# Two transformer blocks in one kernel: the order of work around the gated levels, the latents and the last heads

## The chip, the cores and the metric

One NeuronCore of a Trainium2 chip runs the whole program. It has a matrix engine (TensorE, PE in the profile, with the weight loads as PEld), a vector engine (VectorE, DVE), an activation engine (ScalarE, ACT), GpSimd (POOL) and the queue engine (SyncE, SP). The metric is device microseconds for one execution; lower is better.

## The reference

Two blocks run one after the other on a sequence of 512 tokens of width 1024, all in float32. The first is FFN, a mixer with two recurrences, FFN. The second is FFN, an attention mixer, FFN and a gated embedding. The parts that the change touches, cut from the reference:

```python
# first block, HGRN2 half: 4 heads of 128, chunks of 64
G = jnp.cumsum(gc, axis=2)                                   # log of the forget gates
o_inter = jnp.einsum("bhtk,bhkv->bhtv", qc * jnp.exp(G), S)
rel = G[:, :, :, None, :] - G[:, :, None, :, :]
decay = jnp.exp(jnp.where(causal, rel, -jnp.inf))
scores = jnp.sum(qc[:, :, :, None, :] * kc[:, :, None, :, :] * decay, axis=-1)
o = o_inter + jnp.einsum("bhts,bhsv->bhtv", scores, vc)
S_new = jnp.exp(G_end[:, :, 0, :])[..., None] * S + jnp.einsum("bhsk,bhsv->bhkv", kc * jnp.exp(G_end - G), vc)
...
# second block: latents, 8 softmax heads and 8 stick-breaking heads, branches
proj = u @ w_in[i]
c_q, c_kv, k_rope, sb_qkv, gates = jnp.split(proj, SPLITS, axis=-1)
q = (rms_norm_2(c_q, q_latent_norm[i]) @ w_q_up[i]).reshape(b, s, MLA_HEADS, MLA_QK)
kv = (rms_norm_2(c_kv, kv_latent_norm[i]) @ w_kv_up[i]).reshape(b, s, MLA_HEADS, MLA_NOPE + MLA_V)
o_mla = causal_softmax_attention(...)
o_sb = stick_breaking_attention(sq, sk, sv)
merged = g_mla * (o_mla @ w_branch_mla[i]) + g_sb * (o_sb @ w_branch_sb[i])
h = h + merged @ w_out[i]
```

## The kernel before

**Weights and products.** Every dense product is done as three matmuls on float32r halves (`mm3`: high by high, low by high, high by low). SyncE loads 512 KB pieces of weights ("chunks") into three raw buffers. GpSimd splits each into a high and a low part (`pool_split`, L343 and L345) as soon as TensorE has used up the chunk three places ahead. Each engine's program is written out by hand, in one fixed order, and the engines meet at counting semaphores (`wait_ge`, `then_inc`). A dense product of one chunk is 24 matmuls of 512 columns (L380 to L382).

**The levels of the first mixer.** The decay inside a chunk of 64 steps is cut into seven levels (`level(0)` to `level(6)` on TensorE, L608). Level n reads one of three work buffers, `g.item(n + 1)`. For items 2 to 7 DVE writes the exponents' arguments (`exponents`, L1898 and L1899), ACT takes the exponential (`exponent`, L1379), and DVE multiplies by q and k (`multiply`, L1909 and L1910). After the level's matmuls DVE picks the wanted scores out of PSUM (`keep`, L1920). Between the levels TensorE does the mixer's other dense products (`fill`), and `kv(0, 1)`, `kv(2, 3)`, `kv(4, 5)`, `kv(6)` (L632), the updates of the state. `kv(2, 3)` writes the banks that DVE empties in `remember(0)` and `remember(1)` (L1928, L1933), and waits for both. ACT takes each fill's result out of PSUM (`take`, L1367) between its exponentials, in a fixed order.

**The latents.** The second mixer's input product has 34 chunks (`for i in range(2, 34)` on TensorE, banks 4 to 7 in turn); DVE scales each result into SBUF (L2185). Chunks 0 to 2 are the query latent and 3 and 4 the key and value latent. Their norms need squares (ACT, L1506), sums over partitions on TensorE (`pe_latent_sums`, L816, which waits for each tile of squares), a root and a reciprocal, then a scaled and split copy (`latent_hi` on ACT, L1510). Chunks 18 to 33 are the gates, to which ACT applies a sigmoid (`gate`, L1514).

**The heads.** For each pair of heads TensorE makes stick-breaking logits and sums (L958, L960, L977), softmax logits (L1010), transposes of the divided probabilities (L1022), and the products with the values: `values(h, m)` (L1039 for stick-breaking head h into bank 7, L1042 for softmax head m into bank 6). An odd head uses the upper 64 partitions of its bank, an even one the lower 64. In the loop it is called with m = h - 1; at the end `values(None, 6)` and `values(7, 7)` stand alone. GpSimd divides the probabilities of each head by their row sums (L361). DVE copies the outputs out of PSUM (`stick_out` L2328, `mla_out` L2332). When both heads of a pair are out, ACT makes the high part (L1662) and GpSimd the low part (L355) of the pair's tile for the branch products; DVE makes the low parts of the last two (`last_pairs`, L2346). `pe_merge` then multiplies the eight tiles by each of the 8 branch chunks.

Of the kernel before, what the change touches and what calls it, by code (L numbers as in the profile page):

```python
# [10 lines left out]
ACT = mybir.ActivationFunctionType  # L11
# [3 lines left out]
P = 128  # L15
T = 512
NT = T // P
D = 1024
KD = D // P
# [13 lines left out]
AH = 8  # L33
NOPE, ROPE, QK, HV = 64, 32, 96, 64
KCQ, KCKV = 3, 2
# [207 lines left out]
def tile(t, i):  # L243
    return t[:, i * T:(i + 1) * T]
# [103 lines left out]
def pool_attend(k):  # L348

    pool, H = k.nc.gpsimd, Heads(k)  # L350

    def pairs(h):
        for n in COMPLETE.get(h, ()):
            pool.wait_ge(k.pair_hi, KD + PAIRS.index(n) + 1)
            pool.tensor_tensor(tile(k.ulo, n), H.o[n], tile(k.uhi, n).bitcast(F32), ALU.subtract).then_inc(k.pair_lo, 1)  # L355

    for h in range(AH):
        pool.wait_ge(k.rs_inv, h + 1)
        for i, c in ROWS:
            w = H.probs[:, c:c + (i + 1) * P]  # L360
            d = pool.tensor_scalar(w, w, H.rs[:, h * NT + i:h * NT + i + 1], None, ALU.mult)  # L361
        d.then_inc(k.divided, 1)
        pairs(h)


# [418 lines left out]
def pe_attention_mixer(k):  # L784
    pe = k.nc.tensor
    pe_enter(k, 4, "proj_in")
    for i in range(2, 34):
        if i >= 4:
            pe.wait_ge(k.proj_scaled, i - 3)
        pe_dense(k, "proj_in", i, CHUNK_BANK[i % 4])  # L790
        if i == 8:
            pe_latent_sums(k, 0, KCQ, 0)
        elif i == 11:
            pe_turn_key_rope(k)
        elif i == 18:
            pe_latent_sums(k, KCQ, KCKV, 1)
        elif i == 21:
            pe.wait_ge(k.proj_scaled, 11)
            pe.wait_ge(k.norm_var, NORM["kl"])
            pe.wait_ge(k.kr_step, 1)  # L800
            pe.wait_ge(k.masks_done, 3)
            pe_stick_logits(k, 0)
        elif i == 27:

            pe.wait_ge(k.z_copied, 1)
            pe_turn(k, k.big[:, 14 * T:18 * T], 0, 4 * NT)
    pe_make_heads(k)
    pe_attend(k)
    pe_merge(k)
# [98 lines left out]
def half(h):  # L908
    return slice(h % 2 * HV, (h % 2 + 1) * HV)
# [55 lines left out]
def pe_attend(k):  # L965
# [59 lines left out]
    def values(h, m):  # L1025

        if h is not None:
            pe.wait_ge(k.z_weights, h + 1)
            if h:
                pe.wait_ge(k.z_out, h)  # L1030
        if m is not None:
            pe.wait_ge(k.p_copied, m + 1)
            if m:
                pe.wait_ge(k.o_out, m)
        last = len(CAUSAL_BLOCKS) - 1
        for n, (i, t0, width, c) in enumerate(CAUSAL_BLOCKS):
            if h is not None:
                v = H.sv[:, ((h // 2) * NT + i) * P + h % 2 * HV:((h // 2) * NT + i) * P + (h % 2 + 1) * HV]
                z = pe.matmul(k.ps[7][half(h), t0:t0 + width], v, H.z_at(h, c, width), start=n == 0, stop=n == last, skip_group_check=True)  # L1039
            if m is not None:  # L1040
                v = H.v[:, (m * NT + i) * HV:(m * NT + i + 1) * HV]
                o = pe.matmul(k.ps[6][half(m), t0:t0 + width], v, H.turned_at(m, c, width), start=n == 0, stop=n == last, skip_group_check=True)  # L1042
        if h is not None:
            z.then_inc(k.z_values, 1)
        if m is not None:
            o.then_inc(k.o_values, 1)
# [17 lines left out]
    values(AH - 1, AH - 1)  # L1064


def turned_bank(h):

    return B0 if h < AH - 1 else A0


def pe_merge(k):
    pe = k.nc.tensor
    for j in range(KD):
        n, hi, lo = k.pair("branch", j)
        pe.wait_ge(k.w_split, 2 * n + 2)
        b = 2 * (j % 2)
        if j >= 2:
            pe.wait_ge(k.merge_dve, 3 * (j - 2) + 2)
        else:  # L1080
            pe.wait_ge(k.p_copied, AH)
        for part in (1, 0):
            for t in range(4):
                kk = 4 * part + t
                if j == 0:
                    pe.wait_ge(k.pair_hi, KD + PAIRS.index(kk) + 1)
                    if kk in COMPLETE[AH]:
                        pe.wait_ge(k.last_lo, COMPLETE[AH].index(kk) + 1)
                    else:
                        pe.wait_ge(k.pair_lo, KD + PAIRS.index(kk) + 1)  # L1090
                m = mm3(pe, k.ps[b + part], hi, lo, slice(kk * P, (kk + 1) * P), tile(k.uhi, kk), tile(k.ulo, kk), t == 0, t == 3)
        m.then_inc(k.w_used, 1)

    def ready(kk):
        pe.wait_ge(k.merge_lo, kk + 1)

    def free(i):
        if i == 0:
            pe.wait_ge(k.p_copied, AH)
        elif i == 1:  # L1100
            pe.wait_ge(k.z_out, AH)
            pe.wait_ge(k.o_out, AH)
        else:
            pe.wait_ge(k.merge_dve, 3 * (4 + i) + 2)

    pe_out(k, 4, "proj_out", KD, lambda kk: tile(k.hhi, kk), lambda kk: tile(k.hlo, LO_AT + kk), ready, free, (0, 1, 2, 3))
# [390 lines left out]
def act_attention_mixer(k):  # L1497
# [19 lines left out]
    act_root(k, "ql", k.sc[3][:, :])  # L1517
    for n in range(KCQ):
        latent_hi(n)
    gate(18)  # L1520
    latent_squares(KCQ, KCKV)
    gate(19)
    act_root(k, "kl", k.sc[3][:, :])
    latent_hi(KCQ)
    gate(20)
    latent_hi(KCQ + 1)
    for i in range(21, 34):
        gate(i)
        if i == 21:
# [89 lines left out]
def act_attend(k):  # L1619
# [36 lines left out]
    def pairs(h):  # L1656
        for n in COMPLETE.get(h, ()):
# [3 lines left out]
                act.wait_ge(k.z_out, 2 * n - 6)  # L1661
            act.copy(tile(k.uhi, n), H.o[n]).then_inc(k.pair_hi, 1)  # L1662

    act.preload_act_table_set("natural_log_exp_and_others")
    exponents(0)
    for h in range(1, AH):
        stick_logits(h)
        weigh(h - 1)
        exponents(h)
        act_soft_hi(k, h)  # L1670
        pairs(h)
    weigh(AH - 1)
    pairs(AH)
# [171 lines left out]
def dve_gated_mixer(k):  # L1845
# [108 lines left out]
    dve.wait_ge(k.qf_taken, 8)  # L1954
    dve.tensor_tensor(g.item(1), q, kk, ALU.mult).then_inc(k.level_mul, 1)
    multiply(KEYS_ITEM)
    for n in range(last + 1):
        multiply(n + 2)
        keep(n)
        if n + 3 < QUERIES_ITEM:  # L1960
            exponents(n + 3)
        if n >= 4:
            remember(2 * (n - 4))
            remember(2 * (n - 4) + 1)
# [202 lines left out]
def dve_attention_mixer(k):  # L2167
# [14 lines left out]
    for i in range(34):  # L2182
# [4 lines left out]
        if i == 9:  # L2187
            latent_norm("ql", 0, KCQ, 0)
            latent(0, "q_latent", 0)
        elif i == 10:  # L2190
            latent(1, "q_latent", 1)
            latent(2, "q_latent", 2)
        elif i == 13:
            dve_key_rope(k)
        elif i == 15:
            dve_masks(k)
        elif i == 19:
            latent_norm("kl", KCQ, KCKV, 1)
            latent(3, "kv_latent", 0)
        elif i == 20:  # L2200
            latent(4, "kv_latent", 1)
        elif i == 25:
            dve_softplus(k, 0)
# [93 lines left out]
def dve_attend(k):  # L2297
# [31 lines left out]

    def mla_out(h):  # L2330
        dve.wait_ge(k.o_values, h + 1)
        dve.tensor_copy(H.o[h // 2][half(h), :], k.ps[6][half(h), :]).then_inc(k.o_out, 1)  # L2332

    def split(h):
        dve.wait_ge(k.soft_hi, h + 1)
# [7 lines left out]
    def last_pairs():  # L2343
        for n in COMPLETE[AH]:
            dve.wait_ge(k.pair_hi, KD + PAIRS.index(n) + 1)
            dve.tensor_tensor(tile(k.ulo, n), H.o[n], tile(k.uhi, n).bitcast(F32), ALU.subtract).then_inc(k.last_lo, 1)  # L2346

    split(0)
    maxima(0)
    divide(0)  # L2350
    for h in range(1, AH):
        add_sums(h - 1)
# [207 lines left out]
```

## Time and profile before

| What | Value |
|---|---|
| Time of one execution, median of 3 runs | 2257.95 us (2257.26 to 2259.03) |
| Time of the profiled execution | 2261.95 us |
| Its span | 2260.6 us |
| TensorE busy (matmuls) | 2215.2 us, 98% of the span |
| TensorE weight loads busy | 1832.6 us, 81% |
| GpSimd busy | 1315.4 us, 58% |
| VectorE busy | 828.1 us, 37% |
| ScalarE busy | 452.4 us, 20% |
| Granted TensorE clock, mean | 0.994 |

The span is what the profiler saw between the first and the last instruction; the time of the same execution is 1.35 us more. TensorE is nearly always busy, so the rows that count are those that stand between two of its matmuls, and the stretches in which its granted clock is below 1.00. A row of the timeline gives start, length, engine, line, what it does, and in square brackets how long the engine had been idle before it and who ended that.

### The profile page before, as it was taken

The numbers are of one execution on the slowest core, as the hardware profiler recorded it, in microseconds if no ns is written. First come the engines' busy times: TensorE is split into PE (matmuls) and PEld (weight loads), VectorE is DVE, ScalarE is ACT, GpSimd is POOL, SyncE is SP. The second block draws the span as 40 slices with busy tenths as digits, with TensorE's granted clock in tenths as the row PEclk, the third lists the DMA queues.
The fourth block names the chain that finished last, engine by engine and source line by source line (L and its number), as shares of the span: only waits on it lengthen the run. The fifth ranks groups of instructions, "written<-read, shape, count | busy, mean of one in ns | idle before, by whom it ended". The sixth has DMA issues, their size and how long they took to land.

```text
span 2260.6 us, 25908 instructions
## 1 busy us (share of the span) xinstructions
PE 2215.2 (98%) x10938; PEld 1832.6 (81%) x10938; DVE 828.1 (37%) x929; ACT 452.4 (20%) x751; POOL 1315.4 (58%) x772
## 2 busy tenths in 40 slices
PE   8999999989999999999999999999999999999999
PEld 7888888867788888888888888878767888888887
DVE  3334203776443333104443202143566633333013
ACT  3111004323331111003111102013476121111012
POOL 5666664634356666665666665656435656666654
PEclk9999999999999999999999999999999999999999
DMA  5232322212222323232322322222200323323222
GB/s 182 94 102 93 98 98 75 94 48 66 66 84 99 97 93 102 94 96 82 103 94 95 101 93 94 88 90 84 78 1 20 93 84 100 96 94 111 93 86 92
DMA packets 55819, 200.84 MB, mean 89 GB/s; under 512 B 6680, under 2 KB 6808, under 8 KB 55576
## 3 DMA queue, kind: packets, MB, share of 16 engines
q1 hardware_dynamic: 53856, 194.14, 26.7%
q10 hardware_dynamic: 1848, 5.04, 0.6%
q8 instruction: 87, 1.43, 0.3%
q14 instruction: 28, 0.23, 0.0%
HBM read 197.06 MB, written 2.10 MB: 88 GB/s over the span
## 4 chain that ended last, share of the span: by engine, by line
PE 74%; DVE 2%; ACT 1%; issue 1%; POOL 0%; DVEq 0%; ACTq 0%
PE psum L380 15%; PE psum L382 15%; PE psum L381 15%; PE psum L462 7%; PE psum L463 7%; PE psum L461 7%; PE psum L1010 1%; PE psum L960 1%; PE psum L977 1%; PE psum L425 1%; PE psum L1128 1%; PE psum L1130 1%; PE psum L1129 1%; ACT work L1646 0%; PE psum L668 0%
## 5 line engine op out<-in xcount | busy, mean ns | idle before, releaser
L345 POOL TENSOR_TENSOR w_lo<-w_raw,w_hi 128x1024 fp32r<-128x1024 f32 x365 | 884.2, 2422 | 30.4
L343 POOL TENSOR_SCALAR w_hi<-w_raw 128x1024 fp32r<-128x1024 f32 x365 | 387.3, 1061 | 828.1 <-PE psum L382 573.1
L380 PE MATMUL psum<-u_hi,w_hi 128*128 128x512 f32 (+1 forms) x2072 | 792.8, 383 | 1.9 <-DVE u_lo L1747 1.1
L381 PE MATMUL psum<-u_hi,w_lo 128*128 128x512 f32 (+1 forms) x2072 | 787.9, 380 | 0.0
L382 PE MATMUL psum<-u_lo,w_hi 128*128 128x512 f32 (+1 forms) x2072 | 787.7, 380 | 0.0
L380 PEld LDWEIGHTS psum<-u_hi,w_hi 128*128 128x128 f32 x2072 | 391.6, 189 | 79.2 <-issue 4.7
L382 PEld LDWEIGHTS psum<-u_lo,w_hi 128*128 128x128 f32 x2072 | 391.1, 189 | 74.0
L381 PEld LDWEIGHTS psum<-u_hi,w_lo 128*128 128x128 f32 x2072 | 391.3, 189 | 73.7 <-issue 0.8
L461 PE MATMUL psum<-w_hi,hidden_hi 128*128 128x512 f32 x800 | 311.4, 389 | 0.9 <-DVE work L2099 0.9
L462 PE MATMUL psum<-w_lo,hidden_hi 128*128 128x512 f32 x800 | 311.2, 389 | 0.0
L463 PE MATMUL psum<-w_hi,hidden_lo 128*128 128x512 f32 x768 | 298.8, 389 | 0.0
L1834 DVE TENSOR_TENSOR hidden_lo<-scratch,hidden_hi 128x512 fp32r<-128x512 f32 x88 | 238.3, 2708 | 60.7 <-ACT hidden_hi L1334 60.7
L1832 DVE TENSOR_TENSOR scratch<-scratch,psum 128x512 f32<-128x512 f32 x88 | 60.5, 688 | 404.1 <-PE psum L382 398.9
L461 PEld LDWEIGHTS psum<-w_hi,hidden_hi 128*128 128x128 f32 x800 | 150.1, 188 | 32.6 <-DVE work L2099 1.3
L462 PEld LDWEIGHTS psum<-w_lo,hidden_hi 128*128 128x128 f32 x800 | 150.2, 188 | 31.1
L463 PEld LDWEIGHTS psum<-w_hi,hidden_lo 128*128 128x128 f32 x768 | 144.1, 188 | 29.8
L1334 ACT CAST hidden_hi<-scratch 128x512 fp32r<-128x512 f32 x88 | 54.8, 623 | 406.9 <-DVE scratch L1832 406.9
L1332 ACT ACTIVATE scratch<-scratch 128x512 f32<-128x512 f32 x88 | 55.6, 632 | 394.0 <-DVE scratch L1826 393.9
L1826 DVE TENSOR_TENSOR scratch<-psum,diag 128x512 f32<-128x512 f32 x88 | 60.9, 692 | 121.8 <-PE psum L382 99.9
L1787 DVE SCALAR_TENSOR_TENSOR x<-psum,misc,x 128x1024 f32<-128x1024 f32 x8 | 10.3, 1284 | 223.2 <-PE psum L463 223.1
L1769 DVE SCALAR_TENSOR_TENSOR psum<-psum,misc,post_gain 128x1024 f32<-128x1024 f32 x8 | 10.3, 1293 | 217.3 <-ACT junk L1240 217.0
L1206 ACT ACTIVATE junk<-x 128x1024 bf16<-128x1024 f32 x28 | 29.5, 1052 | 263.5 <-DVE x L1787 252.9
(287 smaller groups left out, 1549.1 us busy)
## 6 DMA issues: line engine op xcount, KB each, us to landing
w_raw<-in_ffn_in SPq DMA_DIRECT2D x176, 512.0 KB, 3.4
w_raw<-in_ffn_out SPq DMA_DIRECT2D x88, 512.0 KB, 3.4
w_raw<-in_proj_in SPq DMA_DIRECT2D x34, 512.0 KB, 3.4
w_raw<-in_mix_in SPq DMA_DIRECT2D x29, 512.0 KB, 3.3
w_raw<-in_embed SPq DMA_DIRECT2D x10, 512.0 KB, 3.5
w_raw<-in_mix_out SPq DMA_DIRECT2D x8, 512.0 KB, 3.4
w_raw<-in_branch SPq DMA_DIRECT2D x8, 512.0 KB, 3.5
w_raw<-in_proj_out SPq DMA_DIRECT2D x8, 512.0 KB, 3.5
```

What stands on the lines that cost most here:

```text
L343: pool.tensor_scalar(hi, raw, 1.0, 1.0, ALU.mult, ALU.mult).then_inc(k.w_split, 1)
L345: pool.tensor_tensor(lo, raw, hi.bitcast(F32), ALU.subtract).then_inc(k.w_split, 1)
L380: pe.matmul(out, hi[:, cols], xhi, start=first, stop=False)
L381: pe.matmul(out, lo[:, cols], xhi, start=False, stop=False)
L382: return pe.matmul(out, hi[:, cols], xlo, start=False, stop=last)
L461: pe.matmul(bank, xhi(kk)[:, tokens], hi[:, cols], start=kk == 0, stop=False)
L462: pe.matmul(bank, xhi(kk)[:, tokens], lo[:, cols], start=False, stop=False)
L463: return pe.matmul(bank, xlo(kk)[:, tokens], hi[:, cols], start=False, stop=last)
L1332: act.activation(sg, sg, ACT.Silu).then_inc(k.silu_done, 1)
L1826: dve.tensor_tensor(sg, k.ps[CHUNK_BANK[2 * i % 4]], k.diag[:, :], ALU.mult).then_inc(k.gate_scaled, 1)
L1832: dve.tensor_tensor(hm, sg, k.ps[CHUNK_BANK[(2 * i + 1) % 4]], ALU.mult).then_inc(k.multiplied, 1)
L1834: dve.tensor_tensor(tile(k.hlo, i), hm, tile(k.hhi, i).bitcast(F32), ALU.subtract).then_inc(k.hid_lo, 1)
```

## The change

Line numbers of the profile are those of the kernel before. Seven edits:

1. DVE writes the exponents' arguments of item n + 3 before it multiplies item n + 2 (from n = 1 on), where it did so after `keep(n)`.
2. The key and value latent's sums on TensorE move from behind chunk 18 to behind chunk 12. On ACT its squares, root and high parts stand together ahead of the gates 18 to 20. On DVE its norm moves from chunk 19 and 20 to chunk 17 and 18.
3. The division of the last softmax head (7) moves from GpSimd to ACT.
4. The last softmax head's output goes to the lower half of bank 5 instead of the upper half of bank 6, so `values(7, 7)` no longer waits for the copy of head 6.
5. `pe_merge` takes the tiles in the order 4, 5, 6, 0, 1, 2, 7, 3 instead of 4, 5, 6, 7, 0, 1, 2, 3.
6. The output product that follows waits for the last head's copy out of bank 5 before it writes there.
7. DVE takes head 0's row maxima before the low part of head 0's sums.

```diff
@@ pool_attend
     for h in range(AH):
-        pool.wait_ge(k.rs_inv, h + 1)
-        for i, c in ROWS:
-            w = H.probs[:, c:c + (i + 1) * P]
-            d = pool.tensor_scalar(w, w, H.rs[:, h * NT + i:h * NT + i + 1], None, ALU.mult)
-        d.then_inc(k.divided, 1)
+
+        if h < AH - 1:
+            pool.wait_ge(k.rs_inv, h + 1)
+            for i, c in ROWS:
+                w = H.probs[:, c:c + (i + 1) * P]
+                d = pool.tensor_scalar(w, w, H.rs[:, h * NT + i:h * NT + i + 1], None, ALU.mult)
+            d.then_inc(k.divided, 1)
         pairs(h)
@@ pe_attention_mixer
-        elif i == 18:
+        elif i == 12:
             pe_latent_sums(k, KCQ, KCKV, 1)
@@ pe_attend, values
             pe.wait_ge(k.p_copied, m + 1)
-            if m:
+            if 0 < m < AH - 1:
                 pe.wait_ge(k.o_out, m)
...
-                o = pe.matmul(k.ps[6][half(m), t0:t0 + width], v, H.turned_at(m, c, width), start=n == 0, stop=n == last, skip_group_check=True)
+                o = pe.matmul(softmax_out(k, m)[:, t0:t0 + width], v, H.turned_at(m, c, width), start=n == 0, stop=n == last, skip_group_check=True)
...
+def softmax_out(k, m):
+
+    return k.ps[6][half(m), :] if m < AH - 1 else k.ps[5][half(0), :]
@@ pe_merge
-        for part in (1, 0):
-            for t in range(4):
-                kk = 4 * part + t
...
+        for kk in (4, 5, 6, 0, 1, 2, 7, 3):
+            part, t = kk // 4, kk % 4
...
     def free(i):
         if i == 0:
-            pe.wait_ge(k.p_copied, AH)
+            pe.wait_ge(k.o_out, AH)
@@ act_attention_mixer
-    gate(18)
     latent_squares(KCQ, KCKV)
-    gate(19)
     act_root(k, "kl", k.sc[3][:, :])
-    latent_hi(KCQ)
-    gate(20)
-    latent_hi(KCQ + 1)
+    for n in range(KCKV):
+        latent_hi(KCQ + n)
+    for i in range(18, 21):
+        gate(i)
@@ act_attend
+    def divide(h):
+        act.wait_ge(k.rs_inv, h + 1)
+        for i, c in ROWS:
+            w = H.probs[:, c:c + (i + 1) * P]
+            a = act.activation(w, w, ACT.Copy, scale=H.rs[:, h * NT + i:h * NT + i + 1])
+        a.then_inc(k.divided, 1)
...
         act_soft_hi(k, h)
+        if h == AH - 1:
+            divide(h)
         pairs(h)
@@ dve_gated_mixer
-    for n in range(last + 1):
+    multiply(2)
+    keep(0)
+    exponents(3)
+    for n in range(1, last + 1):
+        if n + 3 < QUERIES_ITEM:
+            exponents(n + 3)
         multiply(n + 2)
         keep(n)
-        if n + 3 < QUERIES_ITEM:
-            exponents(n + 3)
         if n >= 4:
             remember(2 * (n - 4))
             remember(2 * (n - 4) + 1)
@@ dve_attention_mixer
-        elif i == 19:
+        elif i == 17:
             latent_norm("kl", KCQ, KCKV, 1)
             latent(3, "kv_latent", 0)
-        elif i == 20:
+        elif i == 18:
             latent(4, "kv_latent", 1)
@@ dve_attend
     def mla_out(h):
         dve.wait_ge(k.o_values, h + 1)
-        dve.tensor_copy(H.o[h // 2][half(h), :], k.ps[6][half(h), :]).then_inc(k.o_out, 1)
+        dve.tensor_copy(H.o[h // 2][half(h), :], softmax_out(k, h)).then_inc(k.o_out, 1)
...
+    maxima(0)
     split(0)
-    maxima(0)
     divide(0)
```

What the edits move, engine by engine. VectorE at the levels, before: items are told apart by the shape of their rows, 512x2 is item 3, 256x4 is item 4, 128x8 is item 5; L1898 and L1899 write arguments, L1909 and L1910 multiply, L1920 keeps.

```order
L1898 TENSOR_TENSOR work<-work 128x512x2
L1899 TENSOR_TENSOR work<-work 128x512x2
L1909 TENSOR_TENSOR work<-work 128x512x2
L1910 TENSOR_TENSOR work<-work 128x512x2
L1920 COPY_PREDICATED scratch_f_72<-const,psum 128x1024
L1898 TENSOR_TENSOR work<-work 128x256x4
L1899 TENSOR_TENSOR work<-work 128x256x4
L1909 TENSOR_TENSOR work<-work 128x256x4
L1910 TENSOR_TENSOR work<-work 128x256x4
```

The same place of the changed kernel, where the lines are L1913 and L1914 (arguments), L1924 and L1925 (multiply) and L1935 (keep):

```order
L1913 TENSOR_TENSOR work<-work 128x512x2
L1914 TENSOR_TENSOR work<-work 128x512x2
L1913 TENSOR_TENSOR work<-work 128x256x4
L1914 TENSOR_TENSOR work<-work 128x256x4
L1924 TENSOR_TENSOR work<-work 128x512x2
L1925 TENSOR_TENSOR work<-work 128x512x2
L1935 COPY_PREDICATED scratch_f_72<-const,psum 128x1024
L1913 TENSOR_TENSOR work<-work 128x128x8
L1914 TENSOR_TENSOR work<-work 128x128x8
L1924 TENSOR_TENSOR work<-work 128x256x4
L1925 TENSOR_TENSOR work<-work 128x256x4
```

The arguments of item 4 now stand ahead of the product of item 3, those of item 5 ahead of that of item 4, and so on to item 7.

ScalarE at the latents, before: L1510 is a high part, L1514 a gate, L1506 a square, L1192 the root.

```order
L1510 CAST hidden_lo<-work 128x512 x3
L1514 ACT_TABLE_LOAD
L1514 ACTIVATE work<-work 128x512
L1506 ACTIVATE scratch_66<-work 128x512
L1506 ACTIVATE scratch_67<-work 128x512
L1514 ACTIVATE work<-work 128x512
L1192 ACT_TABLE_LOAD
L1192 ACTIVATE scratch_68<-scratch_68 128x512
L1510 CAST hidden_lo<-work 128x512
L1514 ACT_TABLE_LOAD
```

In the changed kernel (L1517 a high part, L1513 a square, L1199 the root, L1521 a gate):

```order
L1517 CAST hidden_lo<-work 128x512 x3
L1513 ACTIVATE scratch_66<-work 128x512
L1513 ACTIVATE scratch_67<-work 128x512
L1199 ACTIVATE scratch_68<-scratch_68 128x512
L1517 CAST hidden_lo<-work 128x512 x2
L1521 ACT_TABLE_LOAD
L1521 ACTIVATE work<-work 128x512 x4
```

The two squares no longer stand behind gate 18, and two table loads are gone.

ScalarE at the last heads, before: L1616 is the high part of head 7's sums, L1662 the high part of a pair, L1653 the stick-breaking weights of head 7.

```order
L1616 CAST split_sums_63<-scratch_f_72 128x1280
L1662 CAST u_hi<-work 128x512 x2
L1653 ACTIVATE work<-work 128x1280
L1662 CAST u_hi<-work 128x512 x2
```

In the changed kernel (L1622, L1668 and L1659 are those three, L1674 is new):

```order
L1622 CAST split_sums_63<-scratch_f_72 128x1280
L1674 ACTIVATE work<-work,misc 128x512
L1674 ACTIVATE work<-work,misc 128x384
L1674 ACTIVATE work<-work,misc 128x128
L1674 ACTIVATE work<-work,misc 128x256
L1668 CAST u_hi<-work 128x512 x2
L1659 ACTIVATE work<-work 128x1280
L1668 CAST u_hi<-work 128x512 x2
```

Four divisions have come in between the head's sums and the pairs; on GpSimd the four L361 of head 7 are gone.

## Rows read from the trace of the kernel before

**Rows 1.** Waits of TensorE: total us, times, longest.

```profile
PE psum L632 <- DVE work L1933: 5.4, 1, 5.4
...
PE psum L816 <- ACT scratch L1506: 2.0, 1, 2.0
```

**Rows 2.** Timeline of TensorE at the levels: start, us, instruction, idle before.

```profile
463.57 2.09 PE L608 MATMUL psum<-work 128*64 128x64 f32 x64 [3.09 <-DVE work L1910]
...
489.86 2.08 PE L632 MATMUL psum<-work 64*128 64x128 f32 x16 [5.42 <-DVE work L1933]
```

**Rows 3.** Timeline of VectorE at the levels.

```profile
453.83 3.38 DVE L1898 TENSOR_TENSOR work<-work 128x1024 f32<-128x1024 f32 x1
...
460.32 1.23 DVE L1909 TENSOR_TENSOR work<-work 128x1024 f32<-128x1024 f32 x1 [1.98 <-ACT work L1379]
461.46 2.06 DVE L1910 TENSOR_TENSOR work<-work 128x1024 f32<-128x1024 f32 x1
463.44 1.36 DVE L1920 COPY_PREDICATED scratch_f<-const,psum 128x1024 f32<-128x1024 uint32 x1
...
484.63 3.36 DVE L1899 TENSOR_TENSOR work<-work 128x1024 f32<-128x1024 f32 x1
...
488.68 1.12 DVE L1933 SCALAR_TENSOR_TENSOR work<-work,misc,psum 128x128 f32<-128x128 f32 x4
```

**Rows 4.** Timeline of GpSimd beside it.

```profile
453.74 2.38 POOL L345 TENSOR_TENSOR w_lo<-w_raw,w_hi 128x1024 fp32r<-128x1024 f32 x1
```

**Rows 5.** Timeline of ScalarE beside it.

```profile
452.47 0.59 ACT L1367 COPY work<-psum 128x512 f32<-128x512 f32 x1 [2.20 <-PE psum L382]
458.37 1.92 ACT L1379 ACTIVATE work<-work 128x2048 f32<-128x2048 f32 x1 [5.31 <-DVE work L1899]
```

**Rows 6.** Windows of TensorE: us, busy (instructions), granted clock, DMA share, GB/s.

```profile
489.00:496.00 7.00, 6.14 (x26) 0.51 0.09 36
1516.00:1520.00 4.00, 4.00 (x10) 0.57 0.38 131
```

**Rows 7.** Timelines of TensorE, ScalarE and VectorE at the latents.

```profile
1515.17 2.54 PE L816 MATMUL psum<-scratch,const 128*128 128x512 f32 x4 [1.97 <-ACT scratch L1506]
...
1479.11 0.62 ACT L1510 CAST hidden_lo<-work 128x512 fp32r<-128x512 f32 x1 [4.38 <-DVE work L2177]
...
1480.37 1.28 DVE L2185 SCALAR_TENSOR_TENSOR work<-psum,diag 128x512 f32<-128x512 f32 x2
```

**Rows 8.** Timeline of TensorE at the heads 6 and 7.

```profile
1729.55 0.32 PE L1039 MATMUL psum<-work 128*64 128x128 f32 x1
...
1731.66 0.27 PE L1042 MATMUL psum<-work 128*64 128x128 f32 x1
...
1737.46 1.31 PE L1022 MATMUL psum<-const,work 128*128 128x128 f32 x10 [1.09 <-POOL work L361]
1738.70 2.38 PE L1042 MATMUL psum<-work 128*64 128x128 f32 x14
1741.95 0.40 PE L1039 MATMUL psum<-work 128*64 128x128 f32 x2 [0.86 <-DVE work L2332]
...
1746.40 0.50 PE L380 MATMUL psum<-u_hi,w_hi 128*128 128x512 f32 x1
...
1748.59 0.40 PE L380 MATMUL psum<-u_hi,w_hi 128*128 128x512 f32 x1
```

**Rows 9.** Timelines of GpSimd, ScalarE and VectorE beside it.

```profile
1732.79 4.62 POOL L361 TENSOR_SCALAR work<-work,misc 128x512 f32<-128x512 f32 x4 [5.74 <-DVE misc L2341]
...
1733.02 0.64 ACT L1662 CAST u_hi<-work 128x512 fp32r<-128x512 f32 x1
...
1737.93 1.27 ACT L1653 ACTIVATE work<-work 128x1280 f32<-128x1280 f32 x1 [1.14 <-DVE work L2303]
...
1739.95 0.42 DVE L2323 COPY diag<-psum 128x256 f32<-128x256 f32 x1
...
1747.67 1.30 DVE L2346 TENSOR_TENSOR u_lo<-work,u_hi 128x512 fp32r<-128x512 f32 x2
```

More of the change, by code:

```diff
@@ L1081, in pe_merge @@
             pe.wait_ge(k.p_copied, AH)
-        for part in (1, 0):
-            for t in range(4):
-                kk = 4 * part + t
[L1085 to L1091, printed above, removed]
+        for kk in (4, 5, 6, 0, 1, 2, 7, 3):
+            part, t = kk // 4, kk % 4
+            if j == 0:
+                pe.wait_ge(k.pair_hi, KD + PAIRS.index(kk) + 1)
+                if kk in COMPLETE[AH]:
+                    pe.wait_ge(k.last_lo, COMPLETE[AH].index(kk) + 1)
+                else:
+                    pe.wait_ge(k.pair_lo, KD + PAIRS.index(kk) + 1)
+            m = mm3(pe, k.ps[b + part], hi, lo, slice(kk * P, (kk + 1) * P), tile(k.uhi, kk), tile(k.ulo, kk), t == 0, t == 3)
         m.then_inc(k.w_used, 1)
```

## The prediction

> **What bounds the kernel now.** TensorE's matmuls fill 98% of the span, so a change of order can win only what lies between them: waits, and matmuls at the lower clock. I read the waits of TensorE first. In the mixer of the first block one wait of 5.4 us stands out, in front of `kv(2, 3)`; in the second block the longest that this change touches is the 2.0 us in front of the latent sums [rows 1]. Then the timeline of TensorE around them. At the levels it waits 3.09 us for the product of item 4 before `level(3)` at 463.57, and 5.42 us for `remember(1)` before 489.86 [rows 2]. At the last heads it waits 1.09 us for GpSimd's division and 0.86 us for the copy of head 6, and its last pair of products is slow (below) [rows 8]. Third, the windows: after the 5.42 us and after the 1.97 us the granted clock is 0.51 and 0.57, so the engine mostly works at 1.2 instead of 2.4 GHz though it is busy again [rows 6]. The reader is to see that each of these waits costs its own length, and two of them matmuls at half speed behind it.
>
> **Edit 1, arguments ahead of the product.** Before, DVE writes the arguments of an item, then sits idle 1.98 us while ACT takes the exponential, then multiplies [rows 3]. ACT starts when the arguments are there, 458.37 for item 4, though it has been free since 453.06, when it had emptied the fill's bank [rows 5]. With the arguments ahead, those of item 4 are written in the idle time of item 3, which is as long. No split of GpSimd falls there, so two pieces of 1.23 us, overlapped to some 1.15 each (460.32 to 461.46 in the same rows), take 2.3 us in place of 1.98: the product of item 3 ends 0.35 us later, and `level(2)` starts as much later. That is the price. ACT then takes item 4 at 453.06 and is done at 455.0. The arguments of item 5 come next on DVE and meet GpSimd's split of a chunk.
>
> Here VectorE and GpSimd are to be read together [rows 3, 4]: an argument piece that takes 1.21 to 1.23 us alone takes 3.38 us when it starts 0.09 us behind L345 (453.74, 2.38 us long): 2.29 us until that one ends and then its own time, near enough. The split ends at 456.12 plus the shift of 0.35, so the arguments of item 5 end at 456.5 + 2 x 1.2 = 458.9 and the product of item 4 at 461.2, not 463.52. TensorE is ready for `level(3)` at 463.57 - 3.09 + 0.35 = 460.83 and waits about 0.4 us. It starts at 461.2: 2.4 us won. If the two engines shared instead of excluding each other, the arguments, begun at 454.2, would end a microsecond or more sooner, `level(3)` would wait nothing, and the win would be 3.09 - 0.35 = 2.7 us. The Trainium skill, page "SBUF — State Buffer", section on the shared port pair, says that a DVE instruction with two SBUF inputs and a GpSimd one that reads SBUF exclude each other for the whole instruction. It speaks against this edit, since it puts two more such instructions in front of each product; by that rule, the trace agrees and the 2.4 stands.
>
> Next `kv(2, 3)`. It waits for DVE, whose list from 461.2 on is: keep, arguments 6, product 5, keep, arguments 7, product 6, keep, `remember(0)`, `remember(1)`. Dear prices: keep 1.3 (three times), arguments 4.6 (3.38 + 1.23, twice), products 2.3 (twice), `remember(0)` 0.7 (484.63 + 3.36 to 488.68), `remember(1)` 1.1 [rows 3]. Sum 19.5, so 480.7. One product stretched to 3.2 (as in 460.32 to 463.52) gives 481.6. TensorE comes to `kv(2, 3)` at 489.86 - 5.42 - 2.4 = 482.0. The wait is gone with 0.4 to 1.3 us to spare, more if the arguments don't meet a split. So 5.4 us are won, and with them the stretch at half clock: of 489 to 496, 6.14 us were busy at 0.51, and lose 6.14 x 0.49 = 3.0 us [rows 6]. Levels 4 to 6 have their products 1 to 3 us before TensorE is there by the same list. Behind `kv(4, 5)` everything hangs on ACT's bank copies and on TensorE itself, in the same order as before. Edit 1: 2.4 + 5.4 + 3.0 = **10.8 us**.
>
> **Edit 2, latents.** The squares stood behind gate 18 on ACT, which needs chunk 18; TensorE waited for them for 1.97 us and then worked 4.00 us at 0.57 [rows 6, 7]. The second cost is 4.00 x 0.43 = 1.7 us. Now ACT makes them right behind its third high part, from 1479.73 (1479.11 + 0.62); the first is there at 1480.4. TensorE ends chunk 12 at about the time at which DVE is through with chunk 11 and takes 12, 1480.5 to 1481 [rows 7], so it waits 0 to 0.3 us; take 0.1. The sums themselves only move. DVE has the norm two chunks earlier; it will be some 5 us behind with chunk 18, and TensorE asks for that only three chunks later. Gates 18 to 20 come late on ACT, which sat idle most of this stretch. Edit 2: 1.97 + 1.7 - 0.1 = **3.6 us**. If the cover fails (third high part late by the 2.3 us of one split), the wait is back whole: nothing won, bound 0.
>
> **Edits 3 to 6, last heads.** Transposes of head 7: GpSimd's divisions run 1732.79 to 1737.41 [rows 9]; TensorE would be ready at 1737.46 - 1.09 = 1736.37 [rows 8]. On ACT four instructions follow L1616. ACT has no such division in the trace. Below, one instruction of 1280 columns took 1.27 us; above, four times the 0.64 of a 512-column one is 2.6 [rows 9]. I take 1.8, as most of the four are shorter. From 1733.1 that ends at 1734.9, and even the upper bound, 1735.7, is ahead of 1736.37. So 1.09 us go. What ACT holds back by it: pair tile 6, whose low part GpSimd now makes sooner than before, being free of 4.62 us. Then `values(None, 6)` ends at 1740.0, and `values(7, 7)` needs no copy of head 6: weights are there at 1739.2 (1737.93 + 1.27) and the turned probabilities at 1739.3 (1740.37 less the 1.09), so 0.86 us go.
>
> The pair itself: of heads 6 and 5 the 28 matmuls run from 1729.55 to 1731.93, two by two at the same instant, since one head writes the lower and one the upper half of its bank. Those of `values(7, 7)` both write an upper half and run one behind the other from 1741.95 to 1746.40: 4.45 us against 2.38 [rows 8]. With head 7's softmax output in a lower half the pair takes 2.4 us: 2.05 us go. Sum 1.09 + 0.86 + 2.05 = **4.0 us**, and the branches begin at 1742.4.
>
> The Trainium skill, page "TensorE: Matmul & The Clock Gate", Part 3 on packing small matmuls, "What overlaps and what doesn't", would have a weight load overlap a running matmul only if the two use different row groups. Here both heads use all 128 rows, so by that rule the pair would stay at 4.45 us and this part would give 1.95. The trace disagrees: 14 matmuls alone (L1042 at 1738.70) take 2.38 us, as long as the 28 of the pair before.
>
> The branches need tile 7. Its low part followed the last value product by 1.9 us (L2346 at 1747.67, two in 1.30, against 1746.40) [rows 8, 9], and three tiles take 2.2 (1746.40 to the tenth matmul at 1748.59): in the old order it would be a matter of 0.3 us. The new order has six tiles, 4.4 us, ahead of it; even if a GpSimd split of 2.4 us blocks the subtraction it is just there. Edit 5 gives nothing itself, but covers this. Edit 6 waits for something long done. Edit 7: the maxima come a microsecond sooner, but ACT loads a table at that time, so 0.
>
> **Sum.** 10.8 + 3.6 + 4.0 = 18.4 us, from the profiled execution's 2261.95 to 2243.6. The three timed runs have their median 4.0 us below the profiled one, which leaves 2239.6. Part of that 4.0 may be just half-clock stretches, which the timed runs then can't give back; the 1.7 us of the latents followed a wait so short that I count half of it. That and small waits that a list worked out misses make me say **2241 us**.
>
> **The rivals.** (a) As above, 2236 to 2245: chance 0.70. (b) DVE is late after all at `kv(2, 3)`: two products stretched (1.0 us each) and one more argument piece blocked (3.38 for 1.23) take 480.7 to 484.9, a wait of 2.9 us, and the half clock comes back with 3.0 us. That is 2247; for it speaks the slack of 0.4 to 1.3 us, against it that GpSimd has one split of 3.4 us per chunk and can't block every piece. Chance 0.14. (c) The pair of the last heads does not run side by side, or a wait for the copy from the lower to the upper half takes its place: 2.05 us less, 2243; chance 0.05. (d) The latent part does nothing, since the third high part is late, or the clock falls elsewhere instead: 3.5 us less, 2244.5; chance 0.07. (e) The other side: DVE becomes last at each of the levels 2 to 6. Its place is the arguments in front of each product. The price is their whole length, up to 4.6 us, five times, 23 us, and one half-clock stretch of 3.0: 2241 + 26 = 2267. It decides, that is, the kernel is measurably slower, from (2258 + 4.5 - 2241 - 3.0)/5 = 3.7 us per level. Against it: the exponential and DVE's idle 1.98 us per item leave the chain at the same time, and the split blocks one or two pieces per chunk. Chance 0.02. (f) Nothing of it shows, since the waits move to a place that I don't see: 2258; chance 0.02.
>
> **How the numbers follow.** A measurement of this kernel can tell about 0.2%, 4.5 us, from no change. (a) to (d) lie beyond it, which is 0.96; a quarter of a part of (b) and (d) together would fall short, 0.02. So faster 0.94, same 0.04, slower 0.02. The range holds (a), (c), (d) and most of (b): 2235.5 to 2247.5.
>
> **What would show it.** In the profile of the changed kernel: DVE's arguments two rows ahead of the product; no idle time of DVE for the exponential at items 4 to 7; `level(3)` with a wait below 0.5 us; no wait at L632, granted clock 1.00 for the ten microseconds behind it; the latent sums without a wait behind chunk 12; the transposes of head 7 and `values(7, 7)` without waits and the latter's 28 matmuls in 2.4 us; no gap in the first branch product. I am wrong if a wait of more than 2 us stands at L608 or L632 in the levels, or if half-clock stretches as long in sum as before appear elsewhere.

## The result and the profile after

The changed kernel takes 2240.76 us, the median of 4 runs (2239.35 to 2244.82), against 2257.61 us for the kernel before in the same session (2257.18 to 2259.03): ratio 0.9927, 95% interval 0.991 to 0.9944. That is 16.9 us less; the forecast was 2241, with a range of 2235.5 to 2247.5. The profiled execution took 2244.82 us with a span of 2243.5 us, so it is 4.1 us longer than the median.

The page of the changed kernel, first its engines. TensorE is busy 4.0 us less than before, the span is 17.1 us shorter.

```profile
PE 2211.2 (99%) x10938; PEld 1831.7 (82%) x10938; DVE 825.5 (37%) x929; ACT 451.0 (20%) x753; POOL 1314.8 (59%) x768
```

Waits of TensorE in the changed kernel, as [rows 1]. Of the waits that the prediction names, one short one at the levels (L610) is left; those in front of `kv(2, 3)` (now L634), the latent sums (L818), head 7's transposes (L1024) and `values(7, 7)` (L1041) have no row any more.

```profile
PE psum L610 <- DVE work L1925: 0.5, 1, 0.5
```

Timeline of TensorE at the levels, as [rows 2]: levels 2 and 3, `kv(2, 3)`, and L649, the first product behind the levels, which in the kernel before (L647) began at 514.97.

```profile
453.10 2.08 PE L610 MATMUL psum<-work 128*64 128x64 f32 x64 [0.48 <-DVE work L1925]
460.96 2.08 PE L610 MATMUL psum<-work 128*64 128x64 f32 x64
...
481.75 1.16 PE L634 MATMUL psum<-work 64*128 64x128 f32 x16
...
504.07 1.09 PE L649 MATMUL psum<-work,scratch_f 64*64 64x128 f32 x16
```

Timeline of VectorE there, as [rows 3].

```profile
454.24 3.26 DVE L1913 TENSOR_TENSOR work<-work 128x1024 f32<-128x1024 f32 x1
...
458.56 1.21 DVE L1924 TENSOR_TENSOR work<-work 128x1024 f32<-128x1024 f32 x1
459.70 1.21 DVE L1925 TENSOR_TENSOR work<-work 128x1024 f32<-128x1024 f32 x1
...
473.49 1.86 DVE L1924 TENSOR_TENSOR work<-work 128x1024 f32<-128x1024 f32 x1 [1.45 <-ACT work L1386]
...
478.42 1.13 DVE L1948 SCALAR_TENSOR_TENSOR work<-work,misc,psum 128x128 f32<-128x128 f32 x4
482.27 2.28 DVE L1924 TENSOR_TENSOR work<-work 128x1024 f32<-128x1024 f32 x1 [2.73 <-ACT work L1386]
```

Of the arguments of item 5, the first piece (L1913) takes 3.26 us. The product of item 4 (L1924, L1925) stands directly behind them and ends at 460.91; TensorE takes it at 460.96 without a wait. `remember(1)` (L1948) is done at 479.55 and TensorE comes to `kv(2, 3)` at 481.75, 2.2 us later. For items 6 and 7 VectorE still waits for the exponential. Why, the timeline of ScalarE shows:

```profile
468.75 0.59 ACT L1374 COPY work<-psum 128x512 f32<-128x512 f32 x1 [5.46 <-PE psum L384]
469.24 1.08 ACT L1391 COPY work<-psum 128x512 f32<-128x512 f32 x2
...
471.55 1.92 ACT L1386 ACTIVATE work<-work 128x2048 f32<-128x2048 f32 x1
...
479.84 0.59 ACT L1374 COPY work<-psum 128x512 f32<-128x512 f32 x1 [6.24 <-PE psum L384]
480.32 1.92 ACT L1386 ACTIVATE work<-work 128x2048 f32<-128x2048 f32 x1
```

ScalarE starts each exponential (L1386) only when it has emptied the bank of TensorE's fill (L1374), which stands ahead of it in its list; for item 6 four further copies (L1391) stand there too. The arguments are there before that. So ScalarE now waits for TensorE and VectorE for ScalarE; TensorE waits for neither.

At the latents and the heads of the changed kernel, timeline of TensorE, as [rows 7, 8]. The sums run without a wait; the products of `values(7, 7)` (L1041 and L1044, one of each shown) run side by side, and the branches begin at 1729.31.

```profile
1471.00 1.89 PE L818 MATMUL psum<-scratch,const 128*128 128x512 f32 x4
...
1720.86 2.92 PE L979 MATMUL psum<-split_sums,sums_lhs 128*128 128x512 f32 x18 [1.33 <-ACT split_sums L1622]
1723.62 1.28 PE L1024 MATMUL psum<-const,work 128*128 128x128 f32 x10
1724.83 2.27 PE L1044 MATMUL psum<-work 128*64 128x128 f32 x13
...
1728.57 0.27 PE L1041 MATMUL psum<-work 128*64 128x128 f32 x1
1728.67 0.27 PE L1044 MATMUL psum<-work 128*64 128x128 f32 x1
...
1729.31 0.50 PE L382 MATMUL psum<-u_hi,w_hi 128*128 128x512 f32 x1
```

Windows of TensorE in the changed kernel, as [rows 6]: behind level 3, and behind `kv(2, 3)`. Both are at full clock.

```profile
463.50:469.50 6.00, 6.00 (x31) 1.00 0.01 3
488.00:494.00 6.00, 6.00 (x93) 1.00 0.12 27
```

### The profile page after: what moved, and what is told of

Read it like the earlier page. It is cut to its first block, busy times and chain, and to the rows that moved or that the text cites. A ratio compares the mean times of both kernels' runs of the same rounds, so it can differ in the third digit from the quotient of the medians.

```text
span 2243.5 us, 25905 instructions
## 1 busy us (share of the span) xinstructions
PE 2211.2 (99%) x10938; PEld 1831.7 (82%) x10938; DVE 825.5 (37%) x929; ACT 451.0 (20%) x753; POOL 1314.8 (59%) x768
## 4 chain that ended last, share of the span: by engine, by line
PE 93%; DVE 4%; ACT 2%; issue 1%; DMA 0%; POOL 0%; SPq 0%; DVEq 0%; ACTq 0%
PE psum L382 20%; PE psum L384 19%; PE psum L383 19%; PE psum L463 8%; PE psum L464 8%; PE psum L465 8%; PE psum L1012 1%; PE psum L979 1%; PE psum L962 1%; PE psum L427 1%; PE psum L1135 1%; PE psum L1137 1%; PE psum L1136 1%; ACT work L1652 1%; PE psum L610 0%
## 5 line engine op out<-in xcount | busy, mean ns | idle before, releaser
L345 POOL TENSOR_TENSOR w_lo<-w_raw,w_hi 128x1024 fp32r<-128x1024 f32 x365 | 888.2, 2433 | 30.4
```

The lines of the kernel that those rows point to most:

```text
L345: pool.tensor_tensor(lo, raw, hi.bitcast(F32), ALU.subtract).then_inc(k.w_split, 1)
```

## The experiments

The sessions of these runs had medians of 2255.4 to 2257.8 us for the kernel before, and one of them a single run of it at 2254.2. The changed kernel itself was not timed again in them: where a time is set against its 2240.76 us, the two come from different sessions, and a difference of 1 or 2 us between such times shows nothing by itself. Where a stage is compared, its length is read from the trace, since the time of a whole execution also holds half-clock stretches that fall in other places each time (see below).

**Edit 1 undone** in the changed kernel.

```diff
-    multiply(2)
-    keep(0)
-    exponents(3)
-    for n in range(1, last + 1):
+    for n in range(last + 1):
+        multiply(n + 2)
+        keep(n)
         if n + 3 < QUERIES_ITEM:
             exponents(n + 3)
-        multiply(n + 2)
-        keep(n)
```

> The changed kernel with edit 1 alone undone: each item's arguments are written after keep again. If the levels carry 10.8 us as the sum says (2.4 at level 3, 5.4 at kv(2, 3), 3.0 of clock), the time rises from 2240.8 to about 2251.5, with a wait near 3 us at level 3, near 5.4 us at kv(2, 3) and a granted clock near 0.5 behind it. If the clock part is not the wait's doing, both waits come back but only 7.8 us: 2248.5. If the gain came from somewhere else, under 2 us come back.

Measured: 2254.09 us, median of 9 (2244.61 to 2254.88), so 13.3 come back by the medians, where the sum said 10.8. The traced execution was at 2247.33, one of the shorter ones. TensorE's timeline there:

```profile
463.57 2.64 PE L610 MATMUL psum<-work 128*64 128x64 f32 x64 [3.09 <-DVE work L1925]
...
488.19 1.60 PE L634 MATMUL psum<-work 64*128 64x128 f32 x16 [2.19 <-DVE work L1948]
...
512.04 1.09 PE L649 MATMUL psum<-work,scratch_f 64*64 64x128 f32 x16
```

and its windows:

```profile
463.50:469.50 6.00, 5.93 (x74) 0.72 0.29 90
```

The 3.09 us are back, but the 5.42 us are only 2.19. The granted clock fell already behind the wait at level 3 (and again behind `kv(2, 3)`, 0.72 from 488 to 494). That made TensorE 1.5 us later at level 4 (475.12 against 473.59), and with it GpSimd's splits, which follow TensorE. So the split that meets item 7's arguments began 0.18 us behind the first of them, where in the kernel before its second part (L345, 483.72) had begun 0.91 us ahead of the second of them. Timelines of VectorE and GpSimd there:

```profile
483.97 1.21 DVE L1913 TENSOR_TENSOR work<-work 128x1024 f32<-128x1024 f32 x1
...
484.15 3.07 POOL L343 TENSOR_SCALAR w_hi<-w_raw 128x1024 fp32r<-128x1024 f32 x1 [6.76 <-PE psum L384]
```

Now the split is the one that is late, with 3.07 us for a part that takes 1.05 elsewhere, and the arguments took 1.21 and 1.22 us where the second had taken 3.36 [rows 3]. Of the 3.2 us by which the wait is shorter, 1.6 are TensorE's being later and 1.7 VectorE's being sooner (`remember(1)` done at 488.13 against 489.80). The size of this wait is not the program's alone.

**Edit 1 alone** in the kernel before (the same diff the other way).

> The kernel before with edit 1 alone. By the sum 10.8 us less than before, 2257.6 to 2246.8, with no wait at kv(2, 3). If the edits need each other, that is, if the clock or a wait goes only when all are there, the gain is below 8 us: above 2249.5.

Measured: 2247.94 us (2247.79 to 2252.53, 4 runs) against 2257.4, ratio 0.9954 (0.9938 to 0.997): 9.5 us less, no wait at `kv(2, 3)`, L647 at 504.26. The edit needs no other.

**Only `remember` earlier** in the kernel before: it frees what `kv(2, 3)` waits for, but overlaps nothing with the exponential.

```diff
         keep(n)
-        if n + 3 < QUERIES_ITEM:
-            exponents(n + 3)
         if n >= 4:
             remember(2 * (n - 4))
             remember(2 * (n - 4) + 1)
+        if n + 3 < QUERIES_ITEM:
+            exponents(n + 3)
```

> The kernel before, with only remember(0) and remember(1) put ahead of the arguments of items 7 in the list of VectorE; every argument still follows its keep. If the 5.4 us at kv(2, 3) and the 3.0 us of clock behind it are a matter of where remember stands, and the overlap with the exponential is worth only the 2.4 us at level 3, this gives most of the other 8.4: about 2249 to 2251, with the 3.09 us at level 3 left. If the overlap is what frees kv(2, 3), the wait is still above 3 us and the time is within 2 us of before, or a wait for item 7 takes its place at level 6.

Measured: 2257.41 us (11 runs) against 2257.78 (15 runs), ratio 0.9994 (0.9983 to 1.0006): nothing. Its waits at L632 and the next level:

```profile
485.56 1.16 PE L632 MATMUL psum<-work 64*128 64x128 f32 x16 [0.87 <-DVE work L1933]
492.94 2.09 PE L608 MATMUL psum<-work 128*64 128x64 f32 x64 [0.56 <-DVE work L1910]
496.43 1.16 PE L632 MATMUL psum<-work 64*128 64x128 f32 x16 [1.40 <-DVE work L1933]
```

The one wait became three, 2.83 us together. VectorE's list is as long as before, with its idle 1.98 us per item, and what is moved forward makes the next item late. By the medians the theory that the place of `remember` carries 8.4 us fell. Its trace says less against it: the clock stayed full behind level 3, and L647 began at 509.94, that is 5.0 us ahead of the one trace of the kernel before with full clock there (514.97) and 5.9 us behind the changed kernel. In such an execution the overlap carries only the larger part of the gain. Why the medians show none of the 5.0 us is open.

**The kernel before, two more traces**, and **edit 1 undone, a second trace.**

> The kernel before once more, unchanged, for a second trace of it. In the trace of the prediction TensorE waited 5.42 us at kv(2, 3) and lost 3.0 us of clock behind it; in the changed kernel with the levels as before it waited 2.19 us there, after a half-clock stretch behind the wait at level 3. If the wait is fixed by the program, it is 5.4 us here too and the time near 2261. If it depends on where a half-clock stretch happens to fall, a shorter wait shows with a stretch between 464 and 469 us, and the time is near the median, 2257.5.

> The kernel before a third time, for the same question: either 5.4 us at kv(2, 3) with full clock behind level 3, or about 2.2 us with a half-clock stretch behind level 3. A third pattern would speak against both.

> The changed kernel with edit 1 undone, a second trace. Five of its nine executions lay at 2254 to 2255 us, the traced one at 2247.3 with 2.19 us at kv(2, 3). If the long executions are those with the long wait, this run is either near 2254 with 5.4 us at kv(2, 3), or near 2247 with 2.2 us. If it is near 2254 with 2.2 us, the difference lies in half-clock stretches elsewhere in the program.

Measured: 2254.54, 2257.91 and 2245.05 us. TensorE in the second trace of the kernel before (wait at level 3, `kv(2, 3)`, and the end of the levels):

```profile
463.91 3.58 PE L608 MATMUL psum<-work 128*64 128x64 f32 x64 [3.09 <-DVE work L1910]
...
488.47 1.16 PE L632 MATMUL psum<-work 64*128 64x128 f32 x16 [2.19 <-DVE work L1933]
...
510.80 1.09 PE L647 MATMUL psum<-work,scratch_f 64*64 64x128 f32 x16
```

and its windows at level 3:

```profile
463.50:469.50 6.00, 5.59 (x73) 0.72 0.29 90
```

The third trace has the same two waits and a second stretch, 0.72 from 488 to 494; its L647 began at 512.42. In the second trace of the kernel with edit 1 undone, the stretch behind level 3 is longer and the wait at `kv(2, 3)` is gone altogether:

```profile
463.94 3.68 PE L610 MATMUL psum<-work 128*64 128x64 f32 x64 [3.11 <-DVE work L1925]
...
487.30 1.16 PE L634 MATMUL psum<-work 64*128 64x128 f32 x16
...
509.62 1.09 PE L649 MATMUL psum<-work,scratch_f 64*64 64x128 f32 x16
```

Its windows at level 3:

```profile
463.50:469.50 6.00, 5.56 (x69) 0.50 0.29 90
```

In both further traces of the kernel before, too, the split began 0.16 to 0.17 us behind the first arguments of item 7 and was the one held off, and they took 1.21 or 1.22 us each. So the old order has no single price. Its first product behind the levels began at 514.97, 512.04, 510.80, 512.42 and 509.62 in five traces (mean 511.97), that of the new order at 503.92 to 504.55 in eight (504.07 in the changed kernel's own). Edit 1 is worth 5.5 to 10.9 us in these traces, 7.9 on average; the trace that the prediction rests on is the worst of the five. The 7.9 is an average of five traces and not of all executions: the times give 9.5 us for the edit alone and 13.3 for undoing it, and both traces with it undone are of its shorter executions. What remains open is why five of the nine executions of the first experiment lay at 2254 to 2255 us; their mean granted clock is 0.994, against 0.996 in both traced ones, but none of them was traced.

**Edit 2 undone**, and **only the place of the sums as before** (TensorE behind chunk 18, norm at chunks 19 and 20, but ScalarE's order as changed).

```diff
-        elif i == 12:
+        elif i == 18:
             pe_latent_sums(k, KCQ, KCKV, 1)
...
```

> The changed kernel with edit 2 alone undone: sums behind chunk 18, squares behind gate 18. The wait of 1.97 us comes back. If the clock falls with it, as in the kernel before (4.00 us at 0.57), 3.6 us come back: 2244.4; if not, 2.0: 2242.8. The rival that the latents gave nothing says 2240.8.

> The changed kernel with the latent sums of TensorE back behind chunk 18 and the norm back at chunks 19 and 20, but ScalarE's squares still ahead of its gates. If the gate ahead of the squares made the wait, there is none here and the time is that of the changed kernel, 2240.8, within 1. If the place of the sums matters, 2 to 3.6 us come back.

Measured: 2245.66 us (2243.07 to 2248.25, 4 runs) with edit 2 undone, 2240.68 (2237.63 to 2241.01, 5 runs) with only the sums moved back. In the first, TensorE's timeline at the sums:

```profile
1499.31 3.55 PE L818 MATMUL psum<-scratch,const 128*128 128x512 f32 x4 [1.96 <-ACT scratch L1513]
```

and the windows there (us; busy of TensorE, its weight loads, VectorE, ScalarE and GpSimd; granted clock; DMA share; GB/s):

```profile
1499.00:1504.00 5.00, 4.69 (x10) 2.42 (x11) 0.00 (x0) 0.77 (x2) 1.99 (x1) 0.66 0.32 105
```

The wait and the half clock come back together (5.00 x 0.34 = 1.7 us). In the second, ScalarE's timeline has the squares done long before, and TensorE has no wait for them behind chunk 18:

```profile
1466.62 0.62 ACT L1517 CAST hidden_lo<-work 128x512 fp32r<-128x512 f32 x1 [4.40 <-DVE work L2195]
1467.14 1.15 ACT L1513 ACTIVATE scratch<-work 128x512 f32<-128x512 f32 x2
```

The gate ahead of the squares was the whole cause; the move of the sums adds nothing to it. In all six traces with the old order the wait of 1.96 to 1.97 us had a half-clock stretch behind it, in none of the eight others is there one between 1465 and 1520 us. From the first L825 (L827 in the changed kernel) to the first L958 (L960) the six take 60.50 to 60.61 us and the eight 56.67 to 56.71, whether the sums stand behind chunk 18 (56.69) or 12. This part is worth 3.9 us in every traced execution, not in some. Edit 7 was not undone by itself, but other traces can tell: from the first L958 (L960) to head 0's first sum (L977, L979) it is 110.3 us in two traces without the edit (edit 1 alone, the second trace of the kernel before) and in two with it (only the sums moved back, edit 5 undone), all at full clock there. It gives nothing.

**Edits 3 to 6 undone**, then one at a time: GpSimd divides head 7 (edit 3 undone), and head 7's output in an upper half.

```diff
-    return k.ps[6][half(m), :] if m < AH - 1 else k.ps[5][half(0), :]
+    return k.ps[6][half(m), :] if m < AH - 1 else k.ps[5][half(1), :]
```

> The changed kernel with edits 3 to 6 undone. By the sum 4.0 us come back (1.09 at the transposes, 0.86 at the last pair of values, 2.05 because that pair runs one behind the other): 2244.8. The rival that the half of the bank does not matter says 1.95 us: 2242.7.

> The changed kernel with edit 3 alone undone: GpSimd divides head 7. By the sum TensorE waits about 1.1 us again at the transposes of head 7, and 1.1 us come back: 2241.9. If GpSimd's low part of pair 6 then comes late as well, a further wait stands at the branches, up to 2 us more. The rival that ScalarE's division gains nothing says 2240.8.

> The changed kernel, with the last softmax head's output in the upper half of bank 5 instead of the lower. Both heads of the last pair then write upper halves. If the halves decide whether the 28 matmuls run side by side, they take 4.4 us instead of 2.4, and 2.0 us come back: 2242.8. If a weight load overlaps a running matmul only for another row group, the halves do not matter and the time stays 2240.8 with the pair at 2.4 us in both.

Measured: 2243.56 us (2242.08 to 2245.12, 4 runs), 2243.3 (2239.31 to 2247.09, 5 runs) and 2241.62 (2241.21 to 2243.67, 5 runs). These medians lie 2.8, 2.5 and 0.9 us above the changed kernel's, from another session, and the executions scatter by as much as is asked for, so the stage is read: from the first sum of head 7 (L979) to the first branch product. In the changed kernel it is 1729.31 - 1720.86 = 8.45 us. With all undone it is 1726.59 - 1713.46 = 13.13, 4.7 us more; with GpSimd dividing 1728.00 - 1718.10 = 9.90, 1.45 more; with the upper half 10.52, 2.07 more. TensorE in the latter:

```profile
1715.20 2.93 PE L979 MATMUL psum<-split_sums,sums_lhs 128*128 128x512 f32 x18 [1.34 <-ACT split_sums L1622]
...
1725.19 0.38 PE L1041 MATMUL psum<-work 128*64 128x128 f32 x2
1725.41 0.38 PE L1044 MATMUL psum<-work 128*64 128x128 f32 x2
1725.72 0.50 PE L382 MATMUL psum<-u_hi,w_hi 128*128 128x512 f32 x1
```

One head's two matmuls take 0.22 us here and then the other's, where in the changed kernel the two heads start 0.10 us apart and each issues one every 0.11 us. Nothing but the half of the bank differs, and the pair's end is 2.07 us later: the half decides.

**Edit 5 undone.**

```diff
-        for kk in (4, 5, 6, 0, 1, 2, 7, 3):
+        for kk in (4, 5, 6, 7, 0, 1, 2, 3):
```

> The changed kernel with edit 5 alone undone: the branches take tile 7 fourth. The prediction called its cover a matter of 0.3 us, which would give 2241.1. The trace of the changed kernel says more: GpSimd's split of 2.39 us lies ahead of the low parts of the last two tiles, so that of tile 7 is there some 4.0 us after the branches begin, while three tiles take 2.2 us: a wait of about 1.8 us in the first branch product, 2242.6.

Measured: 2242.87 us (2242.71 to 2243.81, 5 runs), 2.1 more than the changed kernel in its session. TensorE's timeline there, in the first branch product:

```profile
1729.49 0.47 PE L382 MATMUL psum<-u_hi,w_hi 128*128 128x512 f32 x1 [1.61 <-DVE u_lo L2364]
```

VectorE's, with the low parts of the last two tiles:

```profile
1726.96 2.98 DVE L2364 TENSOR_TENSOR u_lo<-work,u_hi 128x512 fp32r<-128x512 f32 x2
```

and GpSimd's:

```profile
1726.41 2.38 POOL L345 TENSOR_TENSOR w_lo<-w_raw,w_hi 128x1024 fp32r<-128x1024 f32 x1
```

The low parts start 0.55 us behind a split's second part, and TensorE waits for that of tile 7. In the kernel before the two took 1.30 us [rows 9]. The first branch product, from its first matmul to that of the next one, takes 7.48 us here (1725.52 to 1733.00) and 5.57 in the changed kernel (1729.31 to 1734.88): edit 5 is worth 1.9 us. Counted from the first sum of head 7, the splits begin at 4.75 us in the changed kernel (1725.61 - 1720.86) and at 6.59 with edits 3 to 6 undone (1720.05 - 1713.46), 1.8 us earlier; the branches begin 4.7 us earlier. So edits 3 to 6 bring the low parts 2.9 us nearer, into the second split, and edit 5 covers that.

## Why the prediction was right, and where its steps were off

**The time was right, its make-up less so.** The sum of 18.4 us was 10.8 + 3.6 + 4.0. By the stages it is 7.9 on average + 3.9 + 4.7 = 16.5 us, against 16.9 by the medians. Edit 1 was taken 2.9 us too large against that average, edits 2 to 6 by 1.0 us too small. The prediction took 1.4 us off its gain between the sum (2239.6) and 2241, partly for a reason that does not hold (below). That errors of both signs met within 0.3 us of the median is luck.

**Edit 1: the mechanism right, its size that of one execution.** At level 3 the forecast was 2.4 us, with the product at 461.2; it came at 460.91, and with 0.19 us of price at level 2 (0.48 for 0.29) 2.9 us were won. That is nearer to the 2.7 us of two engines that share than to the 2.4, but the rows are those of exclusion: the first piece of item 5's arguments took 3.26 us and ended 1.09 us behind the end of GpSimd's L345 (454.03, 2.38 us long). The forecast came 0.3 us late mostly because the two pieces behind the split ended 2.23 us after it, not 2.4. Behind it, 5.4 + 3.0 was taken as the program's; it is what one of five traces shows. In the other four the clock falls behind level 3 instead, and the later wait is 2.2 us or none. The sentence in the prediction that the profiled execution's surplus "may be just half-clock stretches, which the timed runs then can't give back" saw the danger, but put it at the latents.

**The spare at `kv(2, 3)`** was forecast at 0.4 to 1.3 us and is 2.2; rival (b) would have needed a VectorE blocked more often. "No idle time of DVE for the exponential at items 4 to 7" is wrong: 1.45 and 2.73 us remain, from ScalarE's fixed order, and cost nothing.

**Edit 2: right** (3.6 us forecast, 3.9 by the stage), and the discount wrong: the prediction counted only half of the 1.7 us, since the wait was "so short". The clock fell in six of six. The wait went by the order on ScalarE alone.

**Edits 3 to 6: right, mis-sized.** The rows' waits (1.09, 0.86) leave out some 0.3 us each: undoing edit 3 alone costs 1.45, not 1.09, and with the other edits undone too it is 3.23 more, of which 2.07 are the pair's and 1.16 stand for the 0.86. Part of that is that a matmul behind a wait no longer overlaps the one ahead; in the changed kernel L1024 begins 0.16 us before the row of L979 ends. ScalarE's four divisions took 1.94 us for the estimated 1.8. The pair gave 2.07 us for 2.05, and rival (c) is refuted. So is what the prediction drew, for this pair, from the rule of the Trainium skill on row groups (page "TensorE: Matmul & The Clock Gate", "What overlaps and what doesn't"), that the halves would not matter: the run with the upper half took 2.07 us more. Edit 5, "a matter of 0.3 us", is the step that failed: it was costed in the old timing, in which no split lay at that place. It is worth 1.9 us (1.61 of them shown as a wait), and without it the 4.7 us would be 2.8.

**Rival (d), the clock falls elsewhere instead,** holds for the profiled execution only. Summing (1 - granted clock) over windows of 2 us, the changed kernel's trace loses 11.9 us and the three of the kernel before 13.6, 8.5 and 11.9. The other seven traces with edit 1 lose 3.4 to 8.6. So the profiled execution, 4.1 us over its median, is one in which the clock fell more often. Its two stretches that neither the trace of before nor most of the others have, in windows of TensorE:

```profile
582.00:586.00 4.00, 4.00 (x11) 0.57 0.26 97
...
1612.00:1617.00 5.00, 4.19 (x18) 0.66 0.34 105
```

## What to carry to other kernels

A wait, and the clock behind it, read from one trace may be one of several courses that the same program takes: trace the kernel several times before a single wait of 5 us is put into a sum, and compare stages by their length, not executions by their time. Where an engine idles for another one's result, issue the next item's input ahead; to move the late consumer forward without that overlap (`remember` alone) shared the lateness out here, and the times showed nothing of it. When an edit brings a stage forward, look again at every piece that was just in time by the old clock, since the other engines' work does not come forward with it.

## What the runs showed of the hardware that was not expected

**The same wait, different answers of the clock.** In six traces of the old order TensorE waited 3.09 to 3.11 us before level 3 with the same work ahead. In two the granted clock stayed at 1.00 behind it, in three it was 0.72 from 463.5 to 469.5, in one 0.50.

**VectorE can hold GpSimd off as well as the reverse.** A split's second part takes 2.40 us (the median of its 365 instructions in the changed kernel). In the changed kernel it began 0.06 us behind the first of four back-to-back VectorE instructions that read two tiles (arguments and product of item 5, 462.10 to 466.71) and took 6.81 us: it ended 2.26 us behind the last of them, as if it had only then begun. Timeline of GpSimd in the changed kernel:

```profile
461.02 1.05 POOL L343 TENSOR_SCALAR w_hi<-w_raw 128x1024 fp32r<-128x1024 f32 x1 [4.60 <-PE psum L384]
462.16 6.81 POOL L345 TENSOR_TENSOR w_lo<-w_raw,w_hi 128x1024 fp32r<-128x1024 f32 x1
468.94 2.02 POOL L343 TENSOR_SCALAR w_hi<-w_raw 128x1024 fp32r<-128x1024 f32 x1
```

The edit makes such series longer, four instructions where there were two and two, so part of the cost of the exclusion goes from VectorE to GpSimd. VectorE's four took 1.21 or 1.22 us each. Here the split was not yet needed and no wait of TensorE followed.
